# Attention in a layer with four token mixers: alternate PSUM banks for narrow units, and the place of the reciprocals

## What is computed

```
s = q @ k.T * scale + bias          # FoX: forget bias; DSA and sliding window: ALiBi
s = where(causal / top-k / window, s, -inf)
p = softmax(s, -1)                  # sliding window: with a sink logit
out = p @ v
```

## Time and profile before

| | |
|---|---|
| median of 3 runs | 1716.51 us (1716.35 to 1718.58) |
| the profiled execution: its own time, its span | 1718.47 us, 1716.6 us |
| PE, DVE, ACT, POOL busy | 97%, 63%, 36%, 48% of the span |
| first FoX half | 256 to 297 us |
| second FoX half with sliding window | 336 to 397 us |
| DSA | 750 to 822 us |

### The profile page before, as it was taken

How to read it: one execution, slowest core, us unless ns; L and a number is a source line. 1 busy time by engine, 2 the same in 40 slices (tenths; PEclk the granted TensorE clock), 3 DMA queues, 4 the chain that set the end, 5 groups by cost and what they waited for, 6 DMA issues and landing times.

```text
span 1716.6 us, 23014 instructions
## 1 busy us (share of the span) xinstructions
PE 1657.1 (97%) x8072; PEld 1356.3 (79%) x8072; DVE 1074.2 (63%) x1852; ACT 612.0 (36%) x1112; POOL 823.7 (48%) x537
## 2 busy tenths in 40 slices
PE   6999998989999999998999999999999999999997
PEld 4877876767888888876788888888888888888886
DVE  7645885676999999478577446643453354345337
ACT  5543236274222222247323454323223222322323
POOL 2521130102446565530487333766557556655855
PEclk9999999999999999999999999999999999999999
DMA  8121131101111111320774422121112012111205
GB/s 346 37 72 52 52 103 41 33 25 47 59 46 46 48 59 43 129 77 2 266 264 138 171 71 77 37 74 49 49 49 73 24 49 73 49 49 49 73 25 208
DMA packets 37601, 138.90 MB, mean 81 GB/s; under 512 B 4640, under 2 KB 4768, under 8 KB 37536
## 3 DMA queue, kind: packets, MB, share of 16 engines
q1 hardware_dynamic: 35296, 130.70, 21.9%
q0 software_dynamic: 2240, 7.34, 1.9%
HBM read 118.10 MB, written 13.63 MB: 77 GB/s over the span
## 4 chain that ended last, share of the span: by engine, by line
PE 83%; DVE 7%; ACT 3%; DMA 2%; issue 1%; SPq 1%; POOL 1%; DVEq 1%; POOLq 0%; ACTq 0%
PE ps L672 25%; PE ps L674 25%; PE ps L673 25%; PE ps L913 2%; PE ps L877 2%; PE ps L799 1%; DMA region_a<-in_x 1%; PE ps L703 1%; DVE region_a L2169 1%; POOL h_t L1635 1%; PE ps L800 1%; DVE region_c L1978 1%; ACT region_a L1370 1%; SPq L559 1%; DMA region_b<-in_w_ada 1%
## 5 line engine op out<-in xcount | busy, mean ns | idle before, releaser
L672 PE MATMUL ps<-h_t,w_t 128*128 128x512 f32 x1112 | 437.0, 393 | 2.0 <-DVE h_t L1970 1.6
L674 PE MATMUL ps<-h_t,w_t 128*128 128x512 f32 x1112 | 433.4, 390 | 0.0
L673 PE MATMUL ps<-h_t,w_t 128*128 128x512 f32 x1112 | 433.3, 390 | 0.0
L672 PEld LDWEIGHTS ps<-h_t,w_t 128*128 128x128 f32 x1112 | 209.2, 188 | 48.8 <-issue 4.3
L1628 POOL TENSOR_TENSOR w_t<-raw,w_t 128x1280 fp32r<-128x1280 f32 (+1 forms) x50 | 141.6, 2832 | 215.5 <-ACT w_t L1210 215.2
L674 PEld LDWEIGHTS ps<-h_t,w_t 128*128 128x128 f32 x1112 | 209.0, 188 | 43.9
L673 PEld LDWEIGHTS ps<-h_t,w_t 128*128 128x128 f32 x1112 | 209.2, 188 | 43.0 <-issue 0.7
L2356 DVE TENSOR_TENSOR y_f<-ps,y_f 128x512 f32<-128x512 f32 x120 | 80.7, 686 | 217.7 <-PE ps L674 217.6
L1787 POOL TENSOR_TENSOR w_t<-raw,w_t 128x512 fp32r<-128x512 f32 x80 | 109.3, 1372 | 139.6 <-ACT w_t L1516 139.6
L2024 DVE MAX8 top<-region_b 128x8 f32<-128x512 f32 (+5 forms) x192 | 159.2, 882 | 19.8 <-issue 19.0
L2027 DVE MATCH_REPLACE8 region_b<-top,region_b 128x512 f32<-128x512 f32 (+5 forms) x192 | 166.3, 876 | 0.0
(11 more groups left out here) (297 smaller groups left out, 3329.9 us busy)
## 6 DMA issues: line engine op xcount, KB each, us to landing
raw<-in_w_ffn SPq DMA_DIRECT2D x46, 512.0 KB, 4.0
raw<-in_w_gates SPq DMA_DIRECT2D x32, 640.0 KB, 4.0
region_b<-in_w_ada SPq DMA_DIRECT2D x33, 512.0 KB, 4.5
region_d<-in_w_ffn SPq DMA_DIRECT2D x20, 512.0 KB, 3.9
raw<-in_w_z SPq DMA_DIRECT2D x18, 512.0 KB, 3.4
region_a<-in_x SPq DMA_DIRECT2D x8, 512.0 KB, 14.9
h_f<-in_w_ada SPq DMA_DIRECT2D x8, 512.0 KB, 8.9
raw<-in_w_o SPq DMA_DIRECT2D x8, 512.0 KB, 3.6
```

What stands on the lines that cost most here:

```text
L672: pe.matmul(o, a_hi, m_hi, start=first, stop=False, skip_group_check=more)
L673: pe.matmul(o, a_hi, m_lo, start=False, stop=False, skip_group_check=more)
L674: return pe.matmul(o, a_lo, m_hi, start=False, stop=last, skip_group_check=more)
```

## The change

It does four things. A unit is called narrow if it is a FoX or DSA unit with b < 4, so that its turned probabilities fit one bank; narrow units are turned into bank 0 or 1 by the parity of u, and if u-1 is narrow too, `turn(u)` waits for the copy of u-2 instead of u-1. PE's loop puts `turn_out(u-1)` ahead of `turn(u)`. DVE's loop puts `group_over_den(u-1)` ahead of `biased(u+1)`, behind `dsa_bias(u+1)`. The twelve semaphores of the blocks T become three, counted in the order 3, 2, 4, 1.

```diff
@@ -426,9 +426,10 @@
         s_act = sem("s_act")
         s_act_hi = sem("s_act_hi")
         s_act_lo = sem("s_act_lo")
-        s_t_sum = {n: sem(f"s_t{n}_sum") for n in (1, 2, 3, 4)}
-        s_t_hi = {n: sem(f"s_t{n}_hi") for n in (1, 2, 3, 4)}
-        s_t_lo = {n: sem(f"s_t{n}_lo") for n in (1, 2, 3, 4)}
+        s_t_sum = sem("s_t_sum")
+        s_t_hi = sem("s_t_hi")
+        s_t_lo = sem("s_t_lo")
+        t_place = {3: 1, 2: 2, 4: 3, 1: 4}
         s_y = sem("s_y")
         s_yf = sem("s_yf")
         s_zero = sem("s_zero")
@@ -482,6 +483,15 @@
 
             at = spare[:, 2 * P:4 * P] if hh == 0 else region_d[:, 2 * hh * P:2 * (hh + 1) * P]
             return at[:, P:2 * P] if b == 0 else at
+
+        def narrow(u):
+            return units[u][0] != "swa" and units[u][1] < HALF // P
+
+        def turned_ps(u):
+
+            if narrow(u):
+                return ps[:, u % 2, :]
+            return ps[:, 0:2, :].rearrange("p a n -> p (a n)")
 
         def logits_ps(u):
             return ps[:, 4 + 2 * (u % 2):6 + 2 * (u % 2), :].rearrange("p a n -> p (a n)")
@@ -870,11 +880,12 @@
                         pe.wait_ge(s_zf, 2 * T_GD)
                 pe.wait_ge(s_exp, u + 1)
                 if u >= 1:
-                    pe.wait_ge(s_pt, u)
+                    pe.wait_ge(s_pt, u - 1 if u >= 2 and narrow(u) and narrow(u - 1) else u)
+                o = turned_ps(u)
                 blocks = [2 * hh + c for hh in range(HEADS) for c in ((0, 1) if b else (1,))] \
                     if kind == "swa" else range(b + 1)
                 for c in blocks:
-                    mm = pe.transpose(ps[:, c // 4, (c % 4) * P:(c % 4 + 1) * P],
+                    mm = pe.transpose(o[:, c * P:(c + 1) * P],
                                       lg[u % 2][:, c * P:(c + 1) * P], ident)
                 mm.then_inc(s_t, 1)
 
@@ -928,11 +939,12 @@
                 for u in range(u0, end):
                     if u + 2 < end:
                         logits(u + 2)
+                    if u > u0:
+                        turn_out(u - 1)
                     turn(u)
                     if u >= end - 2:
                         fill(parts_at[2 * (u - end + 2)])
                     if u > u0:
-                        turn_out(u - 1)
                         values(u - 1)
                     if u >= end - 2:
                         fill(parts_at[2 * (u - end + 2) + 1])
@@ -1145,7 +1157,7 @@
                 if s == 6:
                     pe.wait_ge(s_u, count(i, 12, 6 * g + 2))
                 if s in (1, 3, 4, 5):
-                    pe.wait_ge(s_t_lo[{1: 2, 3: 3, 4: 4, 5: 1}[s]], 1)
+                    pe.wait_ge(s_t_lo, t_place[{1: 2, 3: 3, 4: 4, 5: 1}[s]])
                 m_hi, m_lo = step_moving[s]
                 hi, lo, new = slot_hi[n % SLOTS], slot_lo[n % SLOTS], STEP_NEW[s]
                 for k in range(KT // 2):
@@ -1362,11 +1374,10 @@
                         act.wait_ge(s_pv, group_of(u - 4)[0] + 1)
                     if u == U_DSA + 1:
                         act.wait_ge(s_spill_last, 16)
-                    bank = ps[:, 0:2, :].rearrange("p a n -> p (a n)")
                     if kind == "swa":
-                        dst, src = window_cols(pt[u % 4], b), window_cols(bank, b)
+                        dst, src = window_cols(pt[u % 4], b), window_cols(turned_ps(u), b)
                     else:
-                        dst, src = pt[u % 4][:, 0:(b + 1) * P], bank[:, 0:(b + 1) * P]
+                        dst, src = pt[u % 4][:, 0:(b + 1) * P], turned_ps(u)[:, 0:(b + 1) * P]
                     act.activation(dst, src, ACT.Copy).then_inc(s_pt, 1)
                     if u >= u0 + 2:
                         group_hi(u - 2)
@@ -1586,8 +1597,8 @@
                    .then_inc(s_slot_hi, 1)
 
             def t_hi(T):
-                act.wait_ge(s_t_sum[T], 1)
-                act.activation(t_of[T][0], t_f_of[T][1], ACT.Copy).then_inc(s_t_hi[T], 1)
+                act.wait_ge(s_t_sum, t_place[T])
+                act.activation(t_of[T][0], t_f_of[T][1], ACT.Copy).then_inc(s_t_hi, 1)
 
             first_silu(0)
             first_a_hi(0)
@@ -2178,12 +2189,12 @@
                     dsa_bias(u0)
                 biased(u0)
                 for u in range(u0, end):
-                    if u + 1 < end:
-                        if dsa:
-                            dsa_bias(u + 1)
-                        biased(u + 1)
+                    if u + 1 < end and dsa:
+                        dsa_bias(u + 1)
                     if u > u0:
                         group_over_den(u - 1)
+                    if u + 1 < end:
+                        biased(u + 1)
                     if u >= u0 + 2:
                         group_norm(u - 2)
                     if u >= u0 + 3:
@@ -2285,21 +2296,21 @@
                     order.then_wait(dve.tensor_tensor(o_hi, p_hi, q_hi, ALU.subtract))
                     other = o_hi
                 elif T == 2:
-                    dve.wait_ge(s_t_sum[3], 1)
+                    dve.wait_ge(s_t_sum, t_place[3])
                     (p_hi, other), before = b11_f, t3_f[1]
                     order.then_wait(dve.tensor_tensor(o_lo, before, p_hi, ALU.add))
                 else:
-                    dve.wait_ge(s_t_sum[2], 1)
+                    dve.wait_ge(s_t_sum, t_place[2])
                     (p_hi, other), before = b21_f, t2_f[1]
                     order.then_wait(dve.tensor_tensor(o_lo, p_hi, before, ALU.subtract))
-                dve.tensor_tensor(o_lo, o_lo, other, ALU.add).then_inc(s_t_sum[T], 1)
+                dve.tensor_tensor(o_lo, o_lo, other, ALU.add).then_inc(s_t_sum, 1)
 
             def t_rest(T):
-                dve.wait_ge(s_t_hi[T], 1)
+                dve.wait_ge(s_t_hi, t_place[T])
                 if T in (2, 3):
-                    dve.wait_ge(s_t_sum[{3: 2, 2: 4}[T]], 1)
+                    dve.wait_ge(s_t_sum, t_place[{3: 2, 2: 4}[T]])
                 hi, lo = t_of[T]
-                dve.tensor_tensor(lo, t_f_of[T][1], hi.bitcast(F32), ALU.subtract).then_inc(s_t_lo[T], 1)
+                dve.tensor_tensor(lo, t_f_of[T][1], hi.bitcast(F32), ALU.subtract).then_inc(s_t_lo, 1)
 
             def first_out(q):
                 c, t = down_order(q)
@@ -2330,7 +2341,7 @@
                     order.mark(dve.tensor_tensor(o_hi, p_hi, q_hi, ALU.subtract))
                 elif q == 5:
                     order.wait()
-                    dve.tensor_tensor(o_lo, o_lo, o_hi, ALU.add).then_inc(s_t_sum[1], 1)
+                    dve.tensor_tensor(o_lo, o_lo, o_hi, ALU.add).then_inc(s_t_sum, 1)
                 elif q == 10:
                     t_rest(1)
```

## The result

| | before | after |
|---|---|---|
| median of the runs | 1716.43 us (6 runs) | 1707.04 us (6 runs) |
| range of the runs | 1714.4 to 1718.58 | 1705.7 to 1708.57 |
| profiled execution: own time, span | 1718.47, 1716.6 | 1708.26, 1706.4 |
| mean granted clock of the profiled execution | 0.994 | 0.996 |

The ratio is 0.9946, 95% interval 0.9933 to 0.9959: 9.4 us less, where 7.5 were forecast. 1707.04 lies inside the range.

A forecast was written before the change was run, and what follows sets the result against it. PE was taken as full between and behind the attention stages, with waits only inside them. Gains of 1.8 + 2.8 + 2.8 + 0.15 = 7.55 us, taken as 7.5, from 1716.51 gave 1709.0 us, range 1706.8 to 1712.9.

The forecast's parts named there:

- (a): Wide FoX pairs: turn_out runs inside the next turn's wait for the ACT copy, gaining 1.8 us.
- (b): Narrow FoX pairs: alternate banks remove the turn's idle 0.47 us, gaining 2.8 us, between 0 and 3.3.
- (c): DSA: DVE's reciprocal moves into the gap behind the bias, gaining 2.8 us, between 0 and 3.8.
- the loss at the end: End of DSA: the last pair's turn stands behind turn_out, which needs the reciprocal; 0.5 us late, 0.4 net.
- (d): SWA: turn_out hides in a wait at the end, less small delays; gain 0.15 us, between -2.2 and 0.3.
- (e): Channel sub-layer: merged semaphores are raised and awaited in the same order as before; 0 us.
- Clock: Behind the first FoX half's narrow units: one fall to 1.2 GHz costs 1.5 us; no change of falls counted.
- Rival 1: DSA and SWA: turn_out waits for a late reciprocal and blocks PE; 5 us slower, 1721.6 us; chance 4%.
- the sign that I had named: At each pair, turn_out waits for DVE by more than 0.3 us; this would show the forecast wrong.
- Rival 2: FoX or DSA: only one half works, the other's wait is taken over or stays; 1711.8 us; chance 17%.
- Rival 4: Attention stages: waits are only renamed, gaining 1.8 us in FoX, with a fall more; 1716.2 us; chance 10%.
- Rival 3: PE's clock: a fall less from denser narrow units, 1707.5 us, 14%; or another fall, 1710.5 us, 8%.

The follow-up runs named there:

- experiment 2: Only DVE's new order, reciprocals ahead of the next maximum, against the kernel before: 1710.49 us, ratio 0.9963.
- experiment 4: Both new orders (PE's and DVE's) without alternate banks, against the kernel before: 1709.48 us, ratio 0.9959.
- experiment 1: Only the alternate banks for narrow units, both orders as before, against the kernel before: 1718.38 us, ratio 1.0008.
- experiment 6: Alternate banks and DVE's new order, PE's order as before, against the kernel before: 1707.54 us, ratio 0.994.
- experiment 5: The whole change without its merged semaphores, against the kernel before: 1706.64 us, ratio 0.9942.
- experiment 7: The change, semaphores unmerged, with turn_out ahead of the turn only for wide FoX or DSA units, against the kernel before: 1705.34 us, ratio 0.9927.
- experiment 8: As experiment 7, with DVE's old order kept ahead of sliding-window units, against the kernel before: 1705.73 us, ratio 0.9927.
- experiment 3: Only PE's new order, turn_out ahead of the turn, reciprocals where they were, against the kernel before: 1736.66 us, ratio 1.0117.

## Why the prediction was right

The bound was read rightly: PE stays full between and behind the attention stages, and the 8.8 us of the stages reached the end (v71 to end was 0.18 longer in the first pair of profiles, 0.1 shorter in the second). The terms, one by one:

**(a) and (b), FoX: 4.6 forecast, 2.77 + 2.68 = 5.45 measured.** The intervals between values fell by 0.10, 0.22 and 0.30 in the wide pairs and by 0.93, 0.71 and 0.51 in the three narrow ones of the first half. The wide ones give 0.21 each, near the 0.22 of (a), but by another split: 0.11 is PE's order (experiments 2 and 4), the rest came with DVE's. Only three wide pairs of a half stand behind v1, or v17, so the stages have 1.3 of the 1.8 us of (a); the fourth pair of the second half lies in v15 to v17, which without a fall became 0.07 shorter (47.26 to 47.19). The narrow ones give 0.7 each, where (b) had 0.47, and over both halves 4.2, past even its upper bound of 3.3. The step that failed is "In FoX the idle 0.47 us goes, but turn_out now has no wait to hide in, so only the idle time is gained." I credited the gain to the bank and treated the reciprocal as a small extra of the bound. The experiments show the reverse: the bank alone gives 0.01 at b = 3 (experiment 1); the early reciprocal and turn_out give 0.39 (experiment 4), the bank on top 0.54. The pair took 2.73 instead of the forecast 3.1. The row was there: turn_out in the earlier trace rows starts 0.60 behind the turn of three transposes, and in experiment 6 it starts 0.33 behind the same three, so it was waiting, although no idle time is printed at it.

**(c), DSA: 2.8 forecast, 3.53 measured.** "The alternate banks add nothing in DSA" holds beside both new orders (experiment 4 against 5). The b = 3 pair took 3.60 as forecast, and the loss at the end was 0.39 in the interval, 0.4 forecast. There the turn came 811.23 - 810.39 = 0.84 behind the start of the last bias, before 0.43: 0.41 late, 0.5 forecast. What was too small is the gain per pair: 3.91 over the 13 intervals ahead of the last two, or 0.30 each. The forecast had 3.2 for "15 pairs", but its sum 8 x 0.22 + 6 x 0.24 has only 14 terms, 0.23 each. The seven wide intervals gave 0.26 each, the narrowest 0.40 to 0.45. "In the wide pairs PE's loop binds as well and gains 0.22 by (a)" is half right: of the 0.26, 0.11 is PE's order and the rest DVE's (experiments 6 and 2). That PE's order gives all of it back behind the wide pairs, 0.81 against 0.76, the sum did not have.

**(d), SWA: 0.15 gain forecast, 0.19 loss measured.** Right that the period stays in its middle (three intervals of 10.31 in all before, 10.28 after), wrong in both sizes. PE's order gave 0.11 (42.87 to 42.76, experiment 7 to the change), not 0.3; the wait that turn_out of two transposes moved into is still 0.92 us. The reciprocal ahead of the maximum cost 0.29 (experiment 8), not 0.15.

**(e): nothing**, as forecast (experiment 5).

**Clock.** One fall behind the first half costs 1.56 us (48.82 and 47.26 in the two profiles of before), 1.5 forecast. The first profiles of before and after differ by it, so comparing just those two would have credited the change with 1.6 us too much. Leaving a change of falls out of the sum was right for the stages. For the whole times it is open, as the clocks of experiments 5 to 8 say. In its two profiles the change had no fall behind either FoX half or in DSA, and the one at 260 us in the second stands at a place where before had one too. So the rule of the Trainium skill ("TensorE: Matmul & The Clock Gate", "A second HAM failure mode: psum-queue depth-cycling") is not borne out for the whole change: the narrow units cycle through the banks with short idles and stand at the 2.4 GHz level (1.00 from 292 to 297 in the second profile). By that rule the 1.6 us of the banks would have been paid back, and they were kept. For the banks alone it is not refuted: experiment 1 has a fall at the end of DSA, 6.8 us long, that no other profile has, and three of its 11 runs had mean clocks of 0.990 to 0.993, below all 15 of before beside it. But two of the five runs of experiment 4, without the banks, had 0.993 too.

**Rivals.** Rival 1 is real without DVE's order (+19.8 us in experiment 3). With it what is left is small: the sign that I had named, turn_out waiting over 0.3 us, appeared at seven of DSA's narrow pairs (0.34 to 0.83) and one of FoX, not at each pair, and taking it away gained 0.5 us in DSA (experiment 7), most of it at the last turn. Rivals 2 and 4 did not come. Rival 3, a fall less, stays open: falls come and go by the execution, but they may be fewer in the changed kernel.

By the terms the stages are 1.2 us above the 7.55: 0.85 from FoX, 0.73 from DSA, -0.34 from SWA. The 9.4 us of the medians is past my band of 6 to 9 us and inside the range only because its low end had room for a fall less. By the stages, 8.8, it lies in the band. That it came so near is luck in part: (b) was 1.4 and (c) 0.7 too small, (a) 0.5 (as far as the stages hold it) and (d) 0.3 too large, and (b) rested on the wrong wait.

## What to carry to other kernels

When a transfer looks like the limit of a loop, ask which other wait ends at the same moment, above all where an instruction starts later behind its predecessor than that one needs and prints no idle time: freeing the buffer moved the wait there and gained nothing until the second was gone too. Moving turn_out ahead of the turn paid only where its own operand was early (19.8 us lost otherwise) and the turn still waited (0.11 us a wide pair); where the turn no longer waited it cost 0.12 to 0.19. So choose the order by the width of the unit. Compare stages between fixed points of the work, over two profiles of each kernel, before a difference of 0.1% is put down to a change, and compare whole times at one mean clock.

## What was not expected of the hardware

A fall of PE's clock at a given place of the same program does not come in every execution: behind the first FoX half two executions of the kernel before took 48.82 and 47.26 us. Over the 15 runs of before beside experiments 1 to 4, those with a mean granted clock of 0.997 took 1714.4 to 1716.0 us, those with 0.994 took 1718.7 to 1718.9: some 3.5 us for 0.003. That is most of the kernel's spread. What sets off a fall was not found out.

The three parts are far from additive. Alone, DVE's order gave 6.4 us of gain and PE's order -19.8; the banks gave -1.5, which is not clear of noise (interval 0.9998 to 1.0018) and 0.0 in the FoX halves. That sums to -14.9, and together they gave +9.4. The pair of banks and PE's order without DVE's was not run.
